# Seven-product pairs of a hybrid decoder layer: four block sums rounded and split in one operation each

## The reference, cut to what matters

```python
x = x + 0.5 * swiglu(rmsnorm(x, g_ffn1[i]), w1_gate[i], w1_up[i], w1_down[i])   # D_FF = 5632
h = rmsnorm(x, g_mix[i]); proj = h @ w_in[i]
# latent attention and dilated attention on parts of proj
gates = jax.nn.sigmoid(proj[..., OFF_GATE:].reshape(B, S, N_BRANCH, D_MODEL))
merged = gates[:, :, 0] * (o_mla @ w_br_mla[i]) + gates[:, :, 1] * (o_dil @ w_br_dil[i])
x = x + merged @ w_o[i]
x = x + 0.5 * swiglu(rmsnorm(x, g_ffn2[i]), w2_gate[i], w2_up[i], w2_down[i])
x = x + jax.nn.sigmoid(rmsnorm(x, g_ple[i]) @ w_ple_gate[i]) * (p[i] @ w_ple_proj[i])
```

## Time and profile before

| | |
|---|---|
| median of 3 runs | 2362.2 us (2361.93 to 2362.5) |
| profiled execution, span | 2360.7 us |
| PE busy | 2354.3 us, 10670 matmuls |
| DVE busy | 1908.8 us, 2325 instructions |
| ACT busy | 1504.1 us, 1801 instructions |
| granted clock of PE | nine tenths or more in every slice |

### The profile page before, as it was taken

One profiled execution on the slowest core, in us unless ns is written; L12 is line 12 of the kernel. 1 busy time (PEld: TensorE's weight loads), 2 busy tenths in 40 slices (PEclk: granted clock), 3 DMA queues, 4 the chain that ended last, 5 costly groups with the idle time before them and its releaser, 6 DMA issues.

```text
span 2360.7 us, 28178 instructions
## 1 busy us (share of the span) xinstructions
PE 2354.3 (100%) x10670; PEld 1956.3 (83%) x10670; DVE 1908.8 (81%) x2325; ACT 1504.1 (64%) x1801; POOL 0.4 (0%) x5
## 2 busy tenths in 40 slices
PE   9999999999999999999999999999999999999999
PEld 8888888888888888888888888888888888888887
DVE  6898989798987766657656788888998988897878
ACT  6666666764566665666655666576666666754675
POOL 0000000000000000000000000000000000000000
PEclk9999999999999999999999999999999999999999
DMA  7676767766576654776744777677676777666775
GB/s 248 204 232 198 221 206 218 225 201 211 185 222 182 200 165 143 223 222 205 218 136 130 214 210 209 197 222 206 195 225 206 219 224 223 202 207 197 223 210 178
DMA packets 292098, 481.71 MB, mean 204 GB/s; under 512 B 111160, under 2 KB 113152, under 8 KB 291968
## 3 DMA queue, kind: packets, MB, share of 16 engines
q1 hardware_dynamic: 291520, 479.65, 68.1%
q10 hardware_dynamic: 448, 0.34, 0.1%
HBM read 453.70 MB, written 2.10 MB: 193 GB/s over the span
## 4 chain that ended last, share of the span: by engine, by line
PE 97%; DVE 2%; DMA 1%; ACT 0%; issue 0%; ACTq 0%; DVEq 0%
PE ps L621 37%; PE ps L643 12%; PE ps L644 12%; PE ps L645 12%; PE ps L773 7%; PE ps L775 7%; PE ps L774 7%; PE ps L842 1%; PE ps L858 1%; DVE wl L1714 0%; PE ps L869 0%; PE ps L684 0%; ACT wh L1146 0%; DMA raw<-in_w_ple_proj 0%; DMA raw<-in_w_ple_gate 0%
## 5 line engine op out<-in xcount | busy, mean ns | idle before, releaser
L1714 DVE TENSOR_TENSOR wl<-raw,wh 128x1024 fp32r<-128x1024 f32 x764 | 921.8, 1221 | 351.8 <-ACT wh L1146 346.9
L1146 ACT ACTIVATE wh<-raw 128x1024 fp32r<-128x1024 f32 x763 | 796.6, 1054 | 527.0 <-PE ps L621 227.0
L643 PE MATMUL ps<-wh,hT 128*128 128x512 f32 x1156 | 451.7, 391 | 0.1
L645 PE MATMUL ps<-wh,hT 128*128 128x512 f32 x1156 | 449.9, 389 | 0.0
L644 PE MATMUL ps<-wl,hT 128*128 128x512 f32 x1156 | 449.8, 389 | 0.0
L621 PE MATMUL ps<-wh,hT 128*128 128x512 f32 (+1 forms) x1456 | 392.5, 388 | 0.3 <-DVE vd L2019 0.3
L621 PEld LDWEIGHTS ps<-wh,hT 128*128 128x128 f32 x1456 | 269.1, 188 | 53.5 <-DVE vd L2019 0.5
L643 PEld LDWEIGHTS ps<-wh,hT 128*128 128x128 f32 x1156 | 217.0, 188 | 45.0 <-DVE vd L2019 0.3
L645 PEld LDWEIGHTS ps<-wh,hT 128*128 128x128 f32 x1156 | 217.0, 188 | 45.1
L644 PEld LDWEIGHTS ps<-wl,hT 128*128 128x128 f32 x1156 | 217.1, 188 | 44.4
L621 PE MATMUL ps<-wl,hT 128*128 128x512 f32 x728 | 222.2, 386 | 0.0
(11 more groups left out here) (442 smaller groups left out, 3339.2 us busy)
## 6 DMA issues: line engine op xcount, KB each, us to landing
raw<-in_w_in SPq DMA_DIRECT2D x208, 512.0 KB, 4.1
raw<-in_w_up SPq DMA_DIRECT2D x176, 512.0 KB, 4.6
raw<-in_w_down SPq DMA_DIRECT2D x176, 512.0 KB, 4.5
raw<-in_w_gate SPq DMA_DIRECT2D x175, 512.0 KB, 3.9
raw<-in_w_o SPq DMA_DIRECT2D x32, 512.0 KB, 4.6
raw<-in_w_ple_gate SPq DMA_DIRECT2D x32, 512.0 KB, 4.7
raw<-in_w_br_mla SPq DMA_DIRECT2D x16, 512.0 KB, 4.2
raw<-in_w_br_dil SPq DMA_DIRECT2D x16, 512.0 KB, 4.7
```

Source lines behind the costliest of these rows:

```text
L643: pe.matmul(ps[:, b0 + t, :], xh, wh[:, s, c], start=first, stop=False)
L645: mm = pe.matmul(ps[:, b0 + t, :], xl, wh[:, s, c], start=False, stop=last)
L1146: act.activation(wh[:, j % SLOTS, :], raw[:, j % SLOTS, :], ACT.Copy).then_inc(hi_ready, 1)
L1714: dve.tensor_tensor(wl[:, j % SLOTS, :], raw[:, j % SLOTS, :], wh[:, j % SLOTS, :].bitcast(F32), ALU.subtract).then_inc(lo_ready, 1)
```

## The change

`sums_high` and `sums_rest` treat all four sums (128 x 2048 elements) in one operation each instead of two of 1024. `TH_ready` and `TL_ready` count one a pair, and PE waits once, before product four. ACT waits for the second count of `sums_ready` from the start. `sums_of` itself stays in three operations with two counts. `turn_ends` is one operation over four banks with one count of `ends_ready`; ACT's `silu` now waits for all of it. Other waits are renumbered.

```diff
@@ fast_pair (PE)
-                pe.wait_ge(TL_ready, 2 * count + 1)
+                pe.wait_ge(TL_ready, count + 1)
                 product(b1 + 2, S3, T3, first, last)
                 product(b1 + 3, S1, T1, first, last)
-                pe.wait_ge(TL_ready, 2 * count + 2)
                 product(b1 + 1, S2, T2, first, last)
@@ fast_turn (PE)
-                            pe.wait_ge(ends_ready, 2 * (f * len(FAST_TURNS) + m - 1))
+                            pe.wait_ge(ends_ready, f * len(FAST_TURNS) + m - 1)
@@ gate_up (ACT)
-                            act.wait_ge(ends_ready, 2 * (f * len(FAST_TURNS) + m) - 1)
+                            act.wait_ge(ends_ready, f * len(FAST_TURNS) + m)
@@ sums_high (ACT)
-                for a in range(2):
-                    act.wait_ge(sums_ready, 2 * count + a + 1)
-                    if count and a == 0:
-                        act.wait_ge(fast_done, count - other)
-                    act.activation(dst[:, 2 * a:2 * a + 2, :], src[:, 2 * a:2 * a + 2, :], ACT.Copy).then_inc(TH_ready, 1)
+                act.wait_ge(sums_ready, 2 * count + 2)
+                if count:
+                    act.wait_ge(fast_done, count - other)
+                act.activation(dst[:, :, :], src[:, :, :], ACT.Copy).then_inc(TH_ready, 1)
@@ sums_rest (DVE)
-                for a in range(2):
-                    dve.wait_ge(TH_ready, 2 * count + a + 1)
-                    dve.tensor_tensor(dst[:, 2 * a:2 * a + 2, :], src[:, 2 * a:2 * a + 2, :],
-                                      hi[:, 2 * a:2 * a + 2, :].bitcast(F32), ALU.subtract).then_inc(TL_ready, 1)
+                dve.wait_ge(TH_ready, count + 1)
+                dve.tensor_tensor(dst[:, :, :], src[:, :, :], hi[:, :, :].bitcast(F32), ALU.subtract).then_inc(TL_ready, 1)
@@ turn_ends (DVE)
-                for a in range(2):
-                    dve.tensor_tensor(ends[:, 2 * a:2 * a + 2, :], ps[:, b0 + 2 * a:b0 + 2 * a + 2, :],
-                                      ends[:, 2 * a:2 * a + 2, :], ALU.add).then_inc(ends_ready, 1)
+                dve.tensor_tensor(ends[:, :, :], ps[:, b0:b0 + 4, :], ends[:, :, :], ALU.add).then_inc(ends_ready, 1)
@@ finish_block (DVE)
-                    dve.wait_ge(ends_ready, 2 * (f * len(FAST_TURNS) + m))
+                    dve.wait_ge(ends_ready, f * len(FAST_TURNS) + m)
```

More of the change, by code:

```diff
@@ L736, in last_of_turns @@
                     if j == 4:
-                        pe.wait_ge(ends_ready, 2 * (f + 1) * len(FAST_TURNS))
+                        pe.wait_ge(ends_ready, (f + 1) * len(FAST_TURNS))
                     square_unit(u0 + m * FFN_BODY + j, j, 2 * (j % 8), hTh, hTl, 6 - 2 * (j // 8), KD)
@@ L1777, in gate_up @@
                         sums_of(u0 + target + 1, target % SLOTS,
-                                fasts(f, target // FFN_BODY, FAST_PAIRS.index(target % FFN_BODY // 2)), sums, TL_ready, 2)
+                                fasts(f, target // FFN_BODY, FAST_PAIRS.index(target % FFN_BODY // 2)), sums, TL_ready)
                     if v == 0 and m:
@@ L1824, in half_split, with sums_of @@
                                   ALU.subtract).then_inc(lo_ready, 1)
-            def sums_of(n, s, count, dst, free, halves):
+            def sums_of(n, s, count, dst, free):
                 if count:
-                    dve.wait_ge(free, halves * count)
+                    dve.wait_ge(free, count)
                 dve.wait_ge(raw_in[s + 1], 16 * (n // SLOTS + 1))
@@ L1964, in down @@
                             sums_of(n + SLOTS + 1, target % SLOTS, fasts_down(r, half, target),
-                                    *((sums_d, fast_done, 1) if K == KF else (sums_w, TL_ready, 2)))
+                                    *((sums_d, fast_done) if K == KF else (sums_w, TL_ready)))
                         if half == 0:
@@ L2114, in _ @@
                 if fast_v0(k + SLOTS) and k % 2 == 0:
-                    sums_of(U_V0 + k + SLOTS + 1, k % SLOTS, fasts_v0(k + SLOTS), sums_v, TL_ready, 2)
+                    sums_of(U_V0 + k + SLOTS + 1, k % SLOTS, fasts_v0(k + SLOTS), sums_v, TL_ready)
                 if k == 2 * V0_PAIRS[-1] + 1:
@@ L2394, in _ @@
                     if fast_merge(target) and target % 2 == 0:
-                        sums_of(target + 1, target % SLOTS, fasts_merge(target), sums_m, fast_done, 1)
+                        sums_of(target + 1, target % SLOTS, fasts_merge(target), sums_m, fast_done)
                     if v == 2 * MERGE_PAIRS[-1] + 1:
@@ L2431, in _ @@
                     if fast_ple(j + SLOTS) and j % 2 == 0:
-                        sums_of(U_PLE + j + SLOTS + 1, j % SLOTS, fasts_ple(j + SLOTS), sums_p, TL_ready, 2)
+                        sums_of(U_PLE + j + SLOTS + 1, j % SLOTS, fasts_ple(j + SLOTS), sums_p, TL_ready)
                     if h == 0 and k in (9, 11, 12, 14):
```

## The result

The changed kernel takes 2443.4 us (median of four runs, 2441.96 to 2445.74) where the kernel before takes 2362.1 in the same comparison: a ratio of 1.0346, 95% interval 1.0334 to 1.0358, 81.3 us more. The forecast was 2439.4, 77.2 more. The profiled execution has a span of 2440.2 us, 79.5 over that of before.

What follows compares the result with a forecast made beforehand. PE was taken to bound the kernel, busy 2354.3 of 2360.7 us. Terms 46 + 14 + 8 + 3 + 3 + 0.6 + 2.5 = 77 us, with 1.5 around the span, gave 2439.4 us; range 2413 to 2460.

Steps and rivals of the forecast that it cites:

- The mechanism: In a pair, `TH` waits for all four sums, then `TL` for `TH`; `TL` ends 3.73 us after its old start.
- The turn: FFN turn: pairs late by 0.83, 2.25 and 2.75 us in all; 44.23 instead of 41.62; 46 us over the turns.
- the 0.14 to be saved: Start of an FFN turn: the merged `ends` sum ends in time for PE, which saves 0.14 us.
- Down projections: VectorE falls behind by 1.38 us at pairs without idle time; first halves 14 us, second halves 8 together.
- The lag doesn't build up: Rival, all stages: idle time takes the lag back, each stage pays its largest stall alone; 53 us, 2415; chance 0.14.
- every stall is paid in full: Rival: VectorE's next pair starts from PE's delayed position; a turn costs 4.9 us, total 2490; chance 0.06.
- No stall: Rival: `TL` has over 1.4 us of lead at every pair, so nothing is added; 2359.7 us; chance 0.02.
- faster: Rival: VectorE sets the pace and 118 operations fewer save 0.07 us each, 8 us; 2354; chance 0.01.
- The merge: Merge, nine pairs: only the third of each turn short, by an estimated 1.0 us, three times; 3 us.
- The output projection: Output projection, four pairs: 2.7 us at the last, close behind the one before, 0.3 at the second; 3 us.
- V0 and the last projection: V0, two pairs, 0.6 us; last projection, three pairs at VectorE's own pace, some 2.5 us straight onto the end.
- idle time before `TH`: Sign at PE's first matmul on `TH`, released by `TL`: some 2 us in second pair, 0.5 in first and third.

Runs made afterwards that it cites:

- the late start: Kernel before, except that ScalarE begins either half of `TH` only when all four sums are there; 2386.8 us, ratio 1.0105.

## Why the prediction was right, and where it was off
**The mechanism** was the forecast one. All four steps that it named are in the trace: durations of 1.918 and 2.289 us for 1.91 and 2.28; `TH` 0.04 us behind the fourth sum; 1.38 us of VectorE's idle time in the second and third pair; a turn of 44.20 us for 44.2. The experiments on one part each say the same: release, start and length of the operation each cost something by themselves, and each was put near what it cost, the late start excepted.

**The turn.** Against the trace of before, the shares were 0.69 (0.83 less the 0.14 to be saved), 1.42 and 0.50; measured 0.67, 1.40 and 0.52. That the first fits so well is partly luck: the `ends` sum in one saves PE 0.05 and not 0.14, and a restart costs 0.17 and not 0.22. Sixteen turns of 2.59 make 41.4 us, and the first turns of the two networks 1.9 and 1.0: 44.3, near the 44.0 of the table. The first network's first turn was counted in full and lost 0.7 us less than that; for the second network's 1 us less was allowed, and it was 1.6. That is most of the 2 us under the 46.

**Down projections.** First halves 7.2 us each in the first profiled run of the changed kernel, forecast 7.0 (8.7 in others, where a stretch of slow clock falls into them), so the lag of 1.38 a pair does build up as it was counted. Second halves 6.7 for 8.

**The rivals.** "The lag doesn't build up" needed first halves of 2 us and turns of 2.25; "every stall is paid in full" needed turns of 4.9. Both are refuted by those two numbers. "No stall" and "faster" fall with PE's waits. The second of these was drawn partly from the Trainium skill, VectorE: DVE Perf Modes, in the section on the TRN2 errata. Its duration for 2048 elements is right (2291 ns stated, 2289 measured). The saving worked out from its fixed latency per instruction, 18.5 us for 118 operations, is not there: VectorE's busy time fell by 3.5 us (1908.8 to 1905.3). Operations back to back already overlapped, and even the 0.07 us an operation that this leaves, 8 us in all, came only in part.

**Terms that were mis-sized.**
- The merge: 3 was forecast, 5.4 measured. The step was "only the third of each turn short, by an estimated 1.0". The third pair of each of the three turns is short by 1.63, and the first pair of the second and third turn adds 0.26. `TL_m` of that pair had a distance of 3.13 us: 3.73 - 3.13 leaves 0.60, PE starts 0.06 behind the end of `TL_m`, and the other 0.97 of the 1.63 is a lag that VectorE brings along. VectorE's idle time ahead of the pair was held to take the lag back, but it is idle time for `wh`, and ScalarE is late with `wh` too. VectorE's row there, before and then changed:
```profile
1316.86 1.23 DVE L1714 TENSOR_TENSOR wl<-raw,wh 128x1024 fp32r<-128x1024 f32 x1 [1.45 <-ACT wh L1146]
```
```profile
1351.77 1.23 DVE L1712 TENSOR_TENSOR wl<-raw,wh 128x1024 fp32r<-128x1024 f32 x1 [0.89 <-ACT wh L1145]
```
  Of a lag of 1.5 after the second pair only 0.56 (1.45 less 0.89) was taken back. The wait for `ends_m` that the late start alone shows is not among the changed kernel's waits.
- The output projection: 3 forecast, 4.1 measured, of which 3.4 are at its last pair. The sum for it, 3.73 - 1.50 + 0.3 + 0.2 = 2.7, has the lag of VectorE too small: it is 1.1 and not 0.3. The idle time ahead of the pair shrank from 1.10 to 0.55 us, so that only 0.55 of the lag was taken back, and again it was time for a `wh` that came late as well. Before, changed, and the `TL_w` that PE waits for:
```profile
1536.62 1.22 DVE L1714 TENSOR_TENSOR wl<-raw,wh 128x1024 fp32r<-128x1024 f32 x1 [1.10 <-ACT wh L1146]
```
```profile
1577.81 1.22 DVE L1712 TENSOR_TENSOR wl<-raw,wh 128x1024 fp32r<-128x1024 f32 x1 [0.55 <-ACT wh L1145]
...
1583.60 2.29 DVE L1838 TENSOR_TENSOR TL_w<-sums_w,TH_w 128x2048 fp32r<-128x2048 f32 x1 [1.38 <-ACT TH_w L1280]
```
  PE spends 2.87 us of the 3.4 standing from 1582.85 to 1585.95, and the half microsecond before it at the wait for the half split, for `wl`. The three pairs before add 0.25, 0.35 and 0.13, for which 0.3 was taken.
- The clock: nothing was forecast. It adds 3.2 us behind the output projection in the profiled run, and some 1.6 at each further place where VectorE's lag doesn't cover it.
- V0 and the last projection were put 1.4 us too high together.

So the 77 us came near the 79.5 partly by terms that cancel: the turns, the second halves, V0 and the last projection were 4.7 us too high; the merge, the output projection and the stretch behind it 6.7 too low, the first down halves 0.3. The median is a further 2 us above the profiled run's difference, within the 2441.7 to 2446.1 that the runs of the changed kernel spread over.

**PE's busy time** was expected at about 2354 and is 2381.2 for the same 10670 matmuls. The rows say how. At the second pair PE's last start before the wait is 117.87 and its next 119.36, 1.49 apart, 1.26 more than its rhythm; the bracket shows 1.10 of it, since the matmul before is recorded busy for 0.39 us. The released matmul is recorded with 0.50, and those at the lower clock with 0.63. So the waits of the view, 51.6 us in 74 times, show only two thirds of the 79.5 that were lost, and the rest stands under busy. So the idle time before `TH` that the prediction named as a sign is not there in size: it had some 2 us in the second pair and 0.5 in the first and third, and the brackets show 1.10, 0.45 and 0.22. The 2 us were also at odds with its own sum, in which the second pair adds 1.42. The restart itself was as counted: PE starts 0.06 behind the end of `TL`, and the next step is 0.34 instead of 0.23, 0.17 in all for the forecast's 0.22.

## What to carry to other kernels
Before two operations on a helper engine are merged, take from the timeline how long their first result lies ready before its reader asks, and when the last input of the merged operation exists: here everything beyond that lead was paid by the reader, once for the later release and once for the later start. Do not count on a helper's idle time to take a lag back before you know for whom it waits: where VectorE waited for ScalarE, ScalarE was late as well. Fewer instructions on an engine that doesn't bound the kernel bought nothing here, where merging is harmless only if the reader waits for all parts anyway, as with the `ends` sum. If lead is missing, don't move the reader before you know what it will ask for instead: here that came from the same queue, and the loss in the turns rose from 44 to 76 us.

## What the hardware showed beyond the expected
**PE's clock falls inside a program that is 98% busy.** In the first profiled changed kernel three stretches, the last two microseconds left out, have a granted clock of 0.50, beginning at 544.1 (3.41 us long), 1585.1 (6.83) and 2158.6 (3.41). Each begins next to a place where PE had started no matmul for 2.2 to 3.1 us: from 541.20 to 543.43, from 1582.85 to 1585.95, from 2155.43 to 2157.71. Other gaps of 2.2 to 2.5 us in the same execution are followed by none, and another execution of the same kernel has six such stretches, so it can't be said of a single gap of this length whether it will cost the clock. In the profiled execution of the kernel with only `TH` in one, the longest gaps are 2.04 us and none is followed by such a stretch. At the lower level the matmuls are 0.43 us apart and not 0.227. The Trainium skill, TensorE: Matmul & The Clock Gate, in the section "Wait — 56ns, not 53.3ns?", gives 426.7 and 215.7 ns for this size; the trace agrees with the first and is 11 ns above the second.

The number and place of these stretches differ from run to run. In the profiled executions each stretch that VectorE's lag doesn't cover adds 1.6 to 1.7 us. Most timed runs have no trace, but each has its mean granted clock: 0.995 to 0.998 in all thirteen runs of the changed kernel, which spread over 4.4 us, where the kernel before spreads over 2.0 in fifteen. Within those thirteen the clock does not order the times (2442.4 us at 0.996, 2445.7 at 0.997), so what makes their spread is not shown. With only `TH` in one the four runs are in its order: 2415.8 and 2418.3 us at 1.000, 2418.4 at 0.999, 2422.0 at 0.998. So there too the clock falls in some executions, though not in the profiled one.

**What is left open.** The column of the two FFNs differs by 1.0 us between three executions of the changed kernel (43.9 to 44.9). Most of that lies ahead of the first such pair of the program: 0.0, 0.6 and -0.2 us against before; without it they are 44.0, 44.3 and 44.1. Why the start of the program differs is open, and so is at which gaps of 2.2 to 2.5 us the clock falls.
